# One pair of program copies for experts 3 to 30; the extra-expert lists and the seeding by x1 move to expert 31

## The reference, cut to what matters

```python
logits = (x2 @ w_router + b_router).astype(jnp.float32)
top_vals, top_idx = lax.top_k(logits, TOP_K)
...
for e in range(N_EXPERTS):
    a = clamped_swiglu(x2 @ w_up[e] + b_up[e])
    out = out + combine[:, e:e + 1] * (a @ w_down[e] + b_down[e])
...
return x1 + y
```

## Time and profile before

| | |
|---|---|
| time, median of 3 runs | 1186.02 us |
| the profiled execution | 1184.01 us, span 1181.8 us, mean granted TensorE clock 0.986 |
| TensorE busy | 1140.0 us (96%) |
| VectorE, ScalarE, GpSimd busy | 384.7, 275.5, 81.6 us |
| bytes moved | 449.62 MB, mean 380 GB/s |

### The profile page before, as it was taken

How to read it: one execution, slowest core, us unless ns; L and a number is a source line. 1 busy time by engine, 2 the same in 40 slices (tenths; PEclk the granted TensorE clock), 3 DMA queues, 4 the chain that set the end, 5 groups by cost and what they waited for, 6 DMA issues and landing times.

```text
span 1181.8 us, 13591 instructions
## 1 busy us (share of the span) xinstructions
PE 1140.0 (96%) x5611; PEld 541.8 (46%) x5611; DVE 384.7 (33%) x707; ACT 275.5 (23%) x430; POOL 81.6 (7%) x99
## 2 busy tenths in 40 slices
PE   8999999999999999999999999999999999999997
PEld 7879988885333333333333333333333333333332
DVE  5767865563222222222222322222222212122212
ACT  6765364442111112111111111111111102011001
POOL 7424340000000000000000000000000000000000
PEclk9999999999999999999999999999999999999998
DMA  7464459987999999999999999999999999999995
GB/s 260 171 221 150 157 157 371 388 335 275 426 428 434 434 427 434 433 428 430 437 428 428 435 430 429 433 433 428 433 434 429 431 433 430 430 435 430 428 428 240
DMA packets 39779, 449.62 MB, mean 380 GB/s; under 512 B 3314, under 2 KB 3442, under 8 KB 25540
## 3 DMA queue, kind: packets, MB, share of 16 engines
q1 hardware_dynamic: 38272, 447.75, 90.8%
q10 hardware_dynamic: 1476, 1.42, 0.4%
HBM read 448.12 MB, written 1.05 MB: 380 GB/s over the span
## 4 chain that ended last, share of the span: by engine, by line
PE 67%; DMA 26%; DVE 3%; issue 1%; ACT 1%; POOL 0%; DVEq 0%; another core or an unknown queue 0%; SPq 0%; POOLq 0%; ACTq 0%
PE aux L1774 28%; DMA ring<-w_up_dram 25%; PE acc L1578 12%; PE aux L1849 12%; PE acc L1571 3%; PE aux L1673 3%; PE acc L1757 2%; PE aux L1683 1%; DMA raw<-w_in_dram 1%; DVE w_lo L965 1%; PE aux L1804 1%; PE aux L1831 1%; DVE pick_w L1234 1%; PE aux L1837 1%; DMA x<-x_dram 0%
## 5 line engine op out<-in xcount | busy, mean ns | idle before, releaser
L1774 PE MATMUL aux<-ring,xgT 128*64 128x512 f32 x2048 | 466.1, 605 | 22.2 <-DMA ring<-w_up_dram 21.1
L1774 PEld LDWEIGHTS aux<-ring,xgT 128*64 128x64 f32 x2048 | 147.5, 139 | 313.6 <-issue 266.6
L1849 PE MATMUL aux<-ring,aT 128*64 128x512 f32 x992 | 225.0, 595 | 0.0
L1314 DVE TENSOR_SCALAR glu<-aux 128x512 f32<-128x512 f32 x32 | 22.1, 692 | 372.4 <-PE aux L1774 372.4
L965 DVE TENSOR_TENSOR w_lo<-raw,w_hi 128x1024 fp32r<-128x1024 f32 x80 | 101.5, 1293 | 51.8 <-ACT w_hi L727 51.7
L1849 PEld LDWEIGHTS aux<-ring,aT 128*64 128x64 f32 x992 | 66.7, 136 | 112.3 <-issue 107.3
L909 ACT ACTIVATE sig<-glu 128x512 f32<-128x512 f32 x32 | 20.2, 630 | 393.0 <-DVE glu L1314 393.0
L727 ACT ACTIVATE w_hi<-raw 128x1024 fp32r<-128x1024 f32 x80 | 83.7, 1059 | 88.2 <-PE acc L1578 58.1
L918 ACT ACTIVATE y_hi<-aux,slot_w 128x512 fp32r<-128x512 f32 x31 | 21.3, 687 | 246.8 <-PE aux L1849 246.8
L1578 PE MATMUL acc<-w_hi,hT_hi 128*128 128x512 f32 x188 | 76.3, 406 | 1.3 <-DVE hT_lo L977 1.3
L1578 PE MATMUL acc<-w_lo,hT_hi 128*128 128x512 f32 x188 | 73.8, 393 | 0.0
(11 more groups left out here) (326 smaller groups left out, 1055.9 us busy)
## 6 DMA issues: line engine op xcount, KB each, us to landing
ring<-w_up_dram SPq DMA_DIRECT2D x56, 4096.0 KB, 48.0
ring<-w_down_dram SPq DMA_DIRECT2D x26, 4096.0 KB, 45.5
ring<-w_up_dram SPq DMA_DIRECT2D x15, 2048.0 KB, 10.9
raw<-w_in_dram SPq DMA_DIRECT2D x25, 1024.0 KB, 5.4
ring<-w_down_dram SPq DMA_DIRECT2D x12, 2048.0 KB, 12.5
raw<-w_branch_dram SPq DMA_DIRECT2D x6, 1024.0 KB, 6.6
raw<-w_kv_dram SPq DMA_DIRECT2D x4, 1024.0 KB, 5.1
raw<-w_out_dram SPq DMA_DIRECT2D x4, 1024.0 KB, 5.2
```

The lines of the kernel that those rows point to most:

```text
L1314: nc.vector.tensor_scalar(glu[:], bank_glu[:], LIMIT, None, ALU.min).then_inc(glu_ready, 1)
L1774: ins = nc.tensor.matmul(bank[64 * half:64 * half + 64, :], xgT[:, k], w_rows[:, c0 + half * W:c0 + (half + 1) * W], start=(k == 0), stop= ...
L1849: ins = nc.tensor.matmul(bank[64 * half:64 * half + 64, :], turned[:, j, 64 * ff_half:64 * ff_half + 64], w_rows[:, half * W:(half + 1) * ...
```

## The change: what it does

On TensorE the two written-out items 15 and 16 and the second loop go; the first loop now covers items 3 to 30 (q = 1 to 14), with `rows_apart=True` (one further wait, on a semaphore that was reached long before) in the odd item of every pair. The lists are built in the up stage of item 31. The seeding stands in item 31 behind the gather of item 32, and behind it the wait for `meta`. On DVE one loop covers items 1 to 30, and `list_extras` stands between item 30 and the activation of item 31. No instruction of the arithmetic is added or dropped; SP, ACT and POOL keep their programs.

```diff
-LIST_PAIR = 7
-LIST_ITEM, SEED_ITEM = 2 * LIST_PAIR + 1, 2 * LIST_PAIR + 2
...
-            with dve.Fori(1, LIST_ITEM) as n:
+            with dve.Fori(1, NEXP - 1) as n:
                 item(n)
             list_extras()
-            with dve.Fori(LIST_ITEM, NEXP - 1) as n:
-                item(n)
...
-            def item(n, slot_of, loads, opening=False, seeding=False, listing=False, **special):
-                up_stage(n, slot_of, loads, list_item=listing, **special)
+            def item(n, slot_of, loads, opening=False, **special):
+                up_stage(n, slot_of, loads, **special)
                 if not special.get("first_item"):
                     scatter(n - 1, opening)
-                if seeding:
-                    seed_x1()
                 gather(n + 1)
-                if listing:
-                    pe.wait_ge(meta_ready, 1)
                 turn_activation(n)
...
-            with pe.Fori(1, LIST_PAIR) as q:
+            with pe.Fori(1, NEXP // 2 - 1) as q:
                 item(2 * q + 1, *place_in_pair(q, 0), rows_apart=True)
-                item(2 * q + 2, *place_in_pair(q, 1))
-            item(LIST_ITEM, *place(LIST_ITEM), listing=True)
-            item(SEED_ITEM, *place(SEED_ITEM), seeding=True)
-            with pe.Fori(LIST_PAIR + 1, NEXP // 2 - 1) as q:
-                item(2 * q + 1, *place_in_pair(q, 0))
                 item(2 * q + 2, *place_in_pair(q, 1))
 
             n = NEXP - 1
...
-            up_stage(n, slot_of, loads)
+            up_stage(n, slot_of, loads, list_item=True)
             scatter(n - 1)
             gather(NEXP)
+            seed_x1()
+            pe.wait_ge(meta_ready, 1)
             turn_activation(n)
```

## The result

The changed kernel takes 1189.1 us (median of 9 runs, 1187.89 to 1190.88), the kernel before 1185.91 (9 runs beside it, 1184.13 to 1186.66): ratio 1.0029, 95% interval 1.002 to 1.0037, so +3.4 us (2.4 to 4.4). Slower, as forecast, by 3.4 instead of 5.4 us. The profiled execution of the change took 1190.88, the longest of the nine, with a span of 1189.1.

A forecast was written before the change was run, and what follows sets the result against it. Three parts bound it: TensorE's lead (to 730 us), the transfers' pace (to 1128.90), then a tail of TensorE. 0 + 0 + 1.98 + 3.64 - 0.2 = 5.4 us on 1186.02 gave 1191.4 us, whole range 1188.4 to 1193.4.

The forecast's parts named there:

- the likeliest: The main case, whole kernel: +5.4 us to 1191.4 us, own range 1190.6 to 1192.2, chance 0.68.
- the drop taken away: Rival, item 31: before pays a 1.69 us clock drop that the moved lists remove; +3.7 us, 1189.7, chance 0.12.
- the late last transfers: Rival, last down transfers: they end later than TensorE needs them and hide 2.01 us of moved work; 1189.4, chance 0.08.
- What left items 15 and 16 gains nothing: Items 15 and 16: 6.38 us less work only becomes waiting for transfers; gain 0, far end -6.38.
- TensorE lives on its lead from 300 us on: Up to 730 us: TensorE waits for no transfer; each ordinary item eats 2.7 us of the full ring's lead.
- The program copies cost nothing: Merged loops: branches back and fetching new code cost nothing readable; 0, between -0.26 and 0.
- The lists, 1.98: Item 31: of 2.74 us, 0.76 hides in the wait for the second transfer; 1.98 lands behind it, bounds 1.84 to 3.4.
- The seeding, 3.64: Item 31, between gather and turns: eight matmuls with no transfer to wait for add 3.64 us, bounds 3.4 to 3.7.
- The tail swallows 0.2: Up 32 and last down half: TensorE comes later, so short waits for landings go; 0.2 off, bounds 0 to 0.4.
- Carrying over the 2.01 us: Whole kernel: the profiled execution is 2.01 us below the timed median; that difference was assumed to stay.
- still at about 1128.9: Sign in the changed kernel's profile: item 31's second up half starts where it did before, about 1128.9 us.
- over at 1167: Sign at the end of the changed profile: transfers over at about 1167 us, well before TensorE needs the last chunk.

The follow-up runs named there:

- e3: Kernel before with 24 unread matmuls more (5.35 us) in item 16; 1.0007 of before, +0.8 us (-0.2 to +1.8).
- e2: The change's single pair of program copies, but lists and seeding both in item 2; 1.0019 of before, +2.3 us.
- e10: The change with the seeding in item 2 instead of item 31, lists still in 31; 1.0018 of before, +2.1 us (0.9 to 3.3).
- e1: Kernel before with lists and seeding moved to item 31, keeping both loops and written-out items 15 and 16; 1.0031 of before, +3.7 us.
- e4: Kernel before, unchanged, run and profiled again; 1.0001 of before (0.9993 to 1.001).
- e6: Kernel before with the lists alone moved to item 31, seeding left in item 16; 1.0002 of before, +0.2 us (-0.8 to +1.3).
- e9: Kernel before with the lists moved to item 31 and the seeding to item 28; 1.0011 of before, +1.3 us (0.2 to 2.4).
- e8: Kernel before, unchanged, profiled again; from item 31's second up half to the last scatter 47.23 us.
- e12: Kernel before, unchanged, profiled again; from item 31's second up half to the last scatter 47.27 us.
- e5: Kernel before with four unread matmuls added in item 31's wait for its second transfer; 1.0004 of before, +0.5 us (-0.7 to +1.5).
- e11: Kernel before, unchanged, profiled again; from item 31's second up half to the last scatter 45.94 us.

## Why the prediction was right in its way and 2 us too high

*How the number came out.* 1189.1 lies in the whole range and below the likeliest's own one (1190.6 to 1192.2). The whole range reached that far only because it took in the rivals. Two of them named a time near it: the drop taken away (1189.7), whose condition two of five profiles of before show, and the late last transfers (1189.4), which the same profiles put at 0.4 us at most.

*What left items 15 and 16 gains nothing:* right, by the stretch 650 to 730, and by e3 for most of its 5.35 us. The claim behind it, that TensorE lives on its lead from 300 us on, was too broad: at item 2 the ring covers only some 2 to 3 us (e2, e10). The first wait came three items earlier in the change's profile and two in e1's (691.64), where 2.4 were forecast.

*The program copies cost nothing:* right as far as the runs can tell (e1 against the change, 1.0031 and 1.0029).

*The lists, 1.98:* the mechanism was right, the part before the wait was hidden, and the products stood in the tail. In the rows item 31's second half grew from 7.02 (1128.90 to 1135.92) to 8.77 us (1132.03 to 1140.80): 1.75. DVE and `meta` held up nothing.

*The seeding, 3.64:* the term that was sized wrong, since it counts the matmuls at their full length. They hold TensorE 3.54 us (1143.79 to 1147.33), but they cover a short wait in the turns. In before `turn_weights` began at 1139.69, as soon as VectorE had made `pick_w` (1139.03 + 0.60); in the change VectorE does that while the seeding runs. From the first turn to `turn_gathered` it was 1.49 us (1138.91 to 1140.40) and is 1.11 (1147.33 to 1148.44). Net 3.16. I had looked only at the wait of 0.79 behind the turned tokens, which stayed (0.78), as the prediction says.

*The tail swallows 0.2:* 12.30 became 12.19 us for the up stage of 32, and with the halves of the downs it was 0.34 against this profile of before. So 1.75 + 3.16 - 0.34 = 4.57 in the tail, where the forecast had 5.4. In e4 nothing of this was left to swallow (45.56).

*The clock:* I gave the drop that the change takes away a chance of its own, as if it were in all executions or none. It is in two of five profiles of before, and in none of the five with the lists in item 31 (the change, e1, e6, e9, e10; waits of 0 to 1.28 there). On the mean tails, 50.47 - 46.38 = 4.1 us. Waits of 2.10 (e4) and 2.11 us (e8, e12) at the same place of the same kernel end without and with a drop. That one kernel meets the clock differently from run to run, which the Trainium skill says (TensorE: Matmul & The Clock Gate, What's actually happening), is borne out by these profiles; its reason, a time base that doesn't start with the kernel, no run here shows. That the drop made the measured difference smaller is argued from the profiles; e5, which should have shown it in the time, did not.

*What no step had:* the time outside the span, 0.4 us less. 4.1 - 0.4 = 3.7, against 3.4 (2.4 to 4.4) measured.

*Carrying over the 2.01 us* between the profiled run and the median did no harm: the 2.01 are scatter. Such differences come mainly from where the tail starts, 1128.40 to 1131.05 in before, and from the drop.

*Of the signs,* the start of item 31's second half was not "still at about 1128.9" but at 1132.03, and the transfers were not over at 1167 (DMA share 0.43 from 1166 to 1170). Both are the late landings of this execution, not the change: e1, with the same moves, starts its tail at 1129.13.

## What to carry to other kernels

In a stretch that transfers pace, work on an engine costs little as long as waits of its size still follow before the last transfer that the engine waits for: 1.3 us (0.2 to 2.4) in e9, the lists in its tail included, 0.8 (-0.2 to 1.8) for 5.35 us of matmuls in e3. Behind that point it costs its length, less the short waits that it covers (3.16 of 3.54). So a one-off step here belongs behind the place where the transfers have a queue (not in item 2) and some waits ahead of the last one (three in e9), and not in the last item because that is written out anyway. Before pricing a moved step at its own length, look at the short waits on other engines that it will stand in front of.

## What was unexpected of the hardware

Where the tail starts differs from execution to execution, and most of that is settled some 840 us earlier, ahead of all that the change touches. From 280 to 290 us, where the expert stage begins, the granted clock is 0.83 in three profiles of before (the first, e8, e11) and 0.66 in the two others (e4, e12) and in the change. The first profile of before and the change (columns as in the earlier trace rows):

```profile
280.00:290.00 10.00, 10.00 (x45) 5.51 (x47) 2.20 (x9) 1.87 (x3) 0.00 (x0) 0.83 0.37 130
280.00:290.00 10.00, 10.00 (x41) 5.32 (x40) 1.33 (x6) 1.87 (x3) 0.00 (x0) 0.66 0.30 98
```

The transfers pause there (DMA share 0.37 and 0.30). From 280 to 400 us they run at 397, 395 and 399 GB/s in the first three and at 394, 391 and 390 in e4, e12 and the change. The means differ by 5.3 GB/s; over 120 us that is 0.64 MB, or 1.5 us at 431 GB/s. The tails start at 1128.90, 1129.23 and 1128.40 us in the first three, and at 1130.76, 1131.05 and 1132.03 in the others, 2.4 us later on the mean. No run changed this clock alone, so the link is argued from the traces.

The rest is in how one transfer lands. It is done when the last of its 16 shares has landed, and the shares lie apart by an amount that differs between executions. For item 31's second transfer the landing records of the trace have the first and the last share at 1126.8 and 1128.9 (before), 1126.5 and 1128.4 (e11), 1128.5 and 1131.0 (e12), and 1128.2 and 1132.0 (the change); TensorE went on at 1128.90, 1128.40, 1131.05 and 1132.03. The spread is 1.9 to 3.8 us. In the change the last share came 1.6 us behind the one before it, in before 0.1 us. The rate from 730 to 1100 us is the same in both, 431 GB/s. Together they make the 3.13 us between the two starts, nearly the size of the change's effect, so one pair of profiles (+7.3 us of span) would have misled.
